# An expert loop of a mixture-of-experts trunk: the down projection moved wholly to split float32r products

## The reference

```
def swiglu(h, w_gu, w_down):
    gu = h @ w_gu                      # (rows, 1024) @ (1024, 512)
    g, u = jnp.split(gu, 2, axis=-1)
    return (jax.nn.silu(g) * u) @ w_down   # (rows, 256) @ (256, 1024)

yb = lax.map(expert_block, (xb, blk_e))    # blocks of 128 rows, one expert each
yb = yb * row_g[:, None]
return jnp.zeros((t + 1, d)).at[row_t].add(yb)[:t]
```

## Time and profile before

| | us |
|---|---|
| time, median of 3 runs | 3387.37 |
| lowest, highest | 3383.46, 3392.98 |
| the profiled execution's own time | 3384.38 |
| its span, first to last instruction | 3382.8 |
| expert loop of the first layer, about | 1000 to 1617 of the span |
| expert loop of the second layer, about | 2652 to 3268 of the span |
| mean granted TensorE clock, share of full speed | 0.939 |

### The profile page before, as it was taken

How to read it: one execution, slowest core, us unless ns; L and a number is a source line. 1 busy time by engine, 2 the same in 40 slices (tenths; PEclk the granted TensorE clock), 3 DMA queues, 4 the chain that set the end, 5 groups by cost and what they waited for, 6 DMA issues and landing times. The chain is left out here.

```text
span 3382.8 us, 41792 instructions
## 1 busy us (share of the span) xinstructions
PE 2989.3 (88%) x13540; PEld 2291.4 (68%) x13540; DVE 2044.8 (60%) x2874; ACT 1543.7 (46%) x2382; POOL 578.2 (17%) x561
## 2 busy tenths in 40 slices
PE   2899998899879999999369999988998899999983
PEld 1587776577667777777256877756776677777762
DVE  4544345544458888888345444464445788888854
ACT  0342333332337777777023323243323577777740
POOL 0000000000043333333010000000002343333320
PEclk9899999999889999999669999998998899999985
DMA  8123223123359999998321232321334799999944
GB/s 205 55 88 123 101 100 115 67 85 133 122 191 362 367 368 368 361 361 320 153 69 69 88 137 84 128 80 62 111 106 186 264 364 360 359 370 363 366 162 174
DMA packets 119233, 671.92 MB, mean 199 GB/s; under 512 B 27372, under 2 KB 28652, under 8 KB 84364
## 3 DMA queue, kind: packets, MB, share of 16 engines
q1 hardware_dynamic: 86476, 608.19, 48.9%
q0 software_dynamic: 31456, 57.70, 5.1%
q10 hardware_dynamic: 1152, 4.19, 0.3%
HBM read 655.20 MB, written 56.98 MB: 211 GB/s over the span
## 5 line engine op out<-in xcount | busy, mean ns | idle before, releaser
L1725 DVE TENSOR_TENSOR ew_lo<-ew,e_hi 128x2048 fp32r<-128x2048 f32 x256 | 586.6, 2292 | 189.1 <-ACT e_hi L1584 188.9
L659 PE MATMUL bank<-h_hi,w_hi 128*128 128x512 f32 x1248 | 513.1, 411 | 35.5 <-DVE gt L742 12.1
L1584 ACT ACTIVATE e_hi<-ew 128x2048 fp32r<-128x2048 f32 x256 | 489.9, 1914 | 104.0 <-PE bank L1870 80.1
L659 PE MATMUL bank<-h_hi,w_lo 128*128 128x512 f32 x1248 | 510.0, 409 | 0.0
L659 PE MATMUL bank<-h_lo,w_hi 128*128 128x512 f32 x1248 | 505.4, 405 | 0.0
L593 DVE TENSOR_TENSOR w_lo<-raw,w_hi 128x1024 fp32r<-128x1024 f32 x198 | 242.6, 1225 | 430.6 <-ACT w_hi L585 430.4
L1870 PE MATMUL bank<-e_hi,x_hi 128*128 128x512 f32 x1024 | 413.3, 404 | 0.0
L1870 PE MATMUL bank<-ew_lo,x_hi 128*128 128x512 f32 x1024 | 402.4, 393 | 0.0
L1870 PE MATMUL bank<-e_hi,x_lo 128*128 128x512 f32 x1024 | 400.2, 391 | 0.0
L976 ACT ACTIVATE pr<-sn,negmax 128x256 f32<-128x256 f32 (+3 forms) x256 | 138.4, 541 | 421.2 <-DVE negmax L967 421.2
L1493 POOL DMA_INDIRECT y_d<-y,idx x128 | 217.6, 1700 | 621.5 <-issue 524.0
(11 more groups left out here) (286 smaller groups left out, 4648.6 us busy)
## 6 DMA issues: line engine op xcount, KB each, us to landing
ew<-in_wexp SPq DMA_DIRECT2D x128, 2048.0 KB, 10.1
raw<-in_wmix SPq DMA_DIRECT2D x294, 512.0 KB, 4.0
ew<-in_wexp SPq DMA_DIRECT2D x128, 1024.0 KB, 10.1
yt<-y_d SPq DMA_DIRECT2D x8, 3072.0 KB, 10.1
ada<-in_ada SPq DMA_DIRECT2D x4, 2048.0 KB, 18.2
ew<-in_wexp SPq DMA_DIRECT2D x2, 3072.0 KB, 10.4
h_d<-htok ACTq DMA_DIRECT2D x8, 512.0 KB, 2.6
v_d<-vB SPq DMA_DIRECT2D x1, 3840.0 KB
```

Of the source, the lines that this page charges most:

```text
L659: ins = nc.tensor.matmul(out, lhs, rhs, start=start, stop=stop)
L1584: nc.scalar.activation(e_hi[h][:], up_part(ew, j, h), ACT.Copy).then_inc(whi_done, 1)
L1725: nc.vector.tensor_tensor(up_part(ew_lo, j, h), up_part(ew, j, h), e_hi[h][:].bitcast(F32), ALU.subtract).then_inc(wlo_done, 1)
```

## The change

All 1024 output columns of the down projection are computed with three float32r products instead of one half so and one half plain, 12 products of 512 columns for each expert. The down weights of all columns are split on ScalarE and VectorE, as two pieces of 128x1024 (one for each 128 rows of the contraction) and not one, and this split becomes the first thing that both engines do in a step. `a_hi` is rounded straight from PSUM and `a_lo` subtracted from it; the plain copy `actT` is not made in the loop. Both halves of `y` are copied out by ScalarE, between the first half of `e_hi` and `silu`; VectorE copies none. `sil` and `acted` have one buffer where they had two, so `silu(e)` waits for `gated_up(e-1)`, and `gated_up(e)` for the transposes of e-1. The waits of the other engines follow.

```diff
-            def y_half(eng, it, j):
...
-                    nc.scalar.activation(y[s][:, 0:S], bank[0][:], ACT.Copy).then_inc(yA, 1)
-                else:
-                    nc.vector.tensor_copy(y[s][:, S:D], bank[1][:]).then_inc(yD, 1)
...
                     def scatter(it, j):
                         e, s = 8 * it + j, j % 4
-                        pool.wait_ge(yA, e + 1)
-                        pool.wait_ge(yD, e + 1)
+                        pool.wait_ge(y_copied, 2 * e + 2)
...
                     def turned(it, j):
...
-                        nc.scalar.activation(actT[j % 2][:], G[j % 2][:, 0:2 * BLK].rearrange("p (f t) -> p f t", f=2),
-                                             ACT.Copy).then_inc(at_copied, 1)
-                        act.wait_ge(at_copied, e + 1)
-                        nc.scalar.activation(a_hi[j % 2][:], actT[j % 2][:], ACT.Copy).then_inc(ahi_ready, 1)
+                        nc.scalar.activation(a_hi[j % 2][:], G[j % 2][:, 0:2 * BLK].rearrange("p (f t) -> p f t", f=2),
+                                             ACT.Copy).then_inc(ahi_ready, 1)
+
+                    def down_split(it, j):
+                        e = 8 * it + j
                         act.wait_ge(dw_in[j % 4], 16 * (2 * it + j // 4 + 1))
                         if not (isinstance(e, int) and e == 0):
                             act.wait_ge(dn_ready, e)
-                        nc.scalar.activation(d_hi[:], down_part(ew, j)[:, :, 0:S], ACT.Copy).then_inc(dhi_ready, 1)
+                        for f in range(2):
+                            nc.scalar.activation(d_hi[:, f, :], down_part(ew, j)[:, f, :], ACT.Copy).then_inc(dhi_ready, 1)
+
+                    def y_rows(it, j):
+                        e, s = 8 * it + j, j % 2
+                        act.wait_ge(dn_ready, e + 1)
...
+                        for h, bank in enumerate((SB, (OB, MB))[s]):
+                            nc.scalar.activation(y[s][:, h * S:(h + 1) * S], bank[:], ACT.Copy).then_inc(y_copied, 1)
 
                     def step(it, j, first=False, last=False):
-                        if not (first and j < 2):
-                            y_half(act, it, j - 2)
+                        if not (first and j == 0):
+                            down_split(it, j - 1)
                         if not (last and j == 7):
                             x_half(e + 1, j + 1)
                         if not (first and j == 0):
                             turned(it, j - 1)
                         if not (last and j == 7):
                             w_half(e + 1, it, j + 1, 0)
+                        if not (first and j < 2):
+                            y_rows(it, j - 2)
                         silu(e, j)
...
+                    def down_split(e, j):
+                        for f in range(2):
+                            dve.wait_ge(dhi_ready, 2 * e + f + 1)
+                            nc.vector.tensor_tensor(down_part(ew_lo, j)[:, f, :], down_part(ew, j)[:, f, :],
+                                                    d_hi[:, f, :].bitcast(F32), ALU.subtract).then_inc(dlo_ready, 1)
...
                     def gate_up(e, s):
...
-                            pe.wait_ge(at_copied, e - 1)
+                            pe.wait_ge(alo_ready, e - 1)
...
                     def down(e, s):
                         pe.wait_ge(alo_ready, e + 1)
-                        pe.wait_ge(dlo_ready, e + 1)
                         if not (isinstance(e, int) and e < 2):
-                            pe.wait_ge(yA, e - 1)
-                            pe.wait_ge(yD, e - 1)
+                            pe.wait_ge(y_copied, 2 * e - 2)
...
                         for f in range(2):
-                            for i, (a, w) in enumerate(((a_hi, d_hi[:, f, :]), (a_hi, lo[:, f, 0:S]),
-                                                        (a_lo, d_hi[:, f, :]))):
-                                nc.tensor.matmul(bank[0][:], a[s % 2][:, f, :], w, start=(f, i) == (0, 0),
-                                                 stop=(f, i) == (1, 2))
-                        for f in range(2):
-                            ins = nc.tensor.matmul(bank[1][:], actT[s % 2][:, f, :], raw_w[:, f, S:D], start=f == 0,
-                                                   stop=f == 1)
+                            pe.wait_ge(dlo_ready, 2 * e + f + 1)
+                            for h, bank in enumerate((SB, (OB, MB))[s % 2]):
+                                cols = slice(h * S, (h + 1) * S)
+                                for i, (a, w) in enumerate(((a_hi, d_hi[:, f, cols]), (a_hi, lo[:, f, cols]),
+                                                            (a_lo, d_hi[:, f, cols]))):
+                                    ins = nc.tensor.matmul(bank[:], a[s % 2][:, f, :], w, start=(f, i) == (0, 0),
+                                                           stop=(f, i) == (1, 2))
```

More of the change, by code:

```diff
@@ L314, in hybrid_trunk @@
         x_lo = [place(f"x_lo{i}", [P, KD, BLK], F32R) for i in range(2)]
-        d_hi = place("d_hi", [P, 2, S], F32R)
+        d_hi = place("d_hi", [P, 2, D], F32R)
         xg = [place(f"xg{i}", [P, D]) for i in range(4)]
         y = [place(f"y{i}", [P, D]) for i in range(2)]
-        sil = [place(f"sil{i}", [P, 2 * BLK]) for i in range(2)]
-        acted = [place(f"acted{i}", [P, 2 * BLK]) for i in range(2)]
-        actT = [place(f"actT{i}", [P, 2, BLK]) for i in range(2)]
+        sil = place("sil", [P, 2 * BLK])
+        acted = place("acted", [P, 2 * BLK])
+        actT = place("actT", [P, 2, BLK], at=t_end["acted"] - 8 * BLK)
         a_hi = [place(f"a_hi{i}", [P, 2, BLK], F32R) for i in range(2)]
@@ L1587, in silu @@
                         act.wait_ge(gu_used, 2 * e + 2)
-                        if not (isinstance(e, int) and e < 2):
-                            act.wait_ge(act_done, e - 1)
-                        nc.scalar.activation(sil[j % 2][:], G[j % 2][:, 0:2 * BLK], ACT.Silu).then_inc(silu_done, 1)
+                        if not (isinstance(e, int) and e == 0):
+                            act.wait_ge(act_done, e)
+                        nc.scalar.activation(sil[:], G[j % 2][:, 0:2 * BLK], ACT.Silu).then_inc(silu_done, 1)
                     def turned(it, j):
@@ L1641, in _ @@
                             act.wait_ge(o_gu, i + 1)
-                            nc.scalar.activation(sil[0][:], G[0][:, 0:2 * BLK], ACT.Silu).then_inc(o_sil, 1)
+                            nc.scalar.activation(sil[:], G[0][:, 0:2 * BLK], ACT.Silu).then_inc(o_sil, 1)
                             act.wait_ge(o_dn, i + 1)
@@ L1729, in gated_up @@
                         dve.wait_ge(silu_done, e + 1)
-                        if not (isinstance(e, int) and e < 2):
-                            dve.wait_ge(at_ready, e - 1)
-                        nc.vector.scalar_tensor_tensor(acted[j % 2][:], sil[j % 2][:], idx[j % 8][:, 2:3].bitcast(F32),
+                        if not (isinstance(e, int) and e == 0):
+                            dve.wait_ge(at_ready, e)
+                        nc.vector.scalar_tensor_tensor(acted[:], sil[:], idx[j % 8][:, 2:3].bitcast(F32),
                                                        G[j % 2][:, 2 * BLK:], ALU.mult, ALU.mult).then_inc(act_done, 1)
@@ L1736, in turned @@
                         dve.wait_ge(ahi_ready, e + 1)
-                        nc.vector.tensor_tensor(a_lo[j % 2][:], actT[j % 2][:], a_hi[j % 2][:].bitcast(F32),
-                                                ALU.subtract).then_inc(alo_ready, 1)
-                        dve.wait_ge(dhi_ready, e + 1)
-                        nc.vector.tensor_tensor(down_part(ew_lo, j)[:, :, 0:S], down_part(ew, j)[:, :, 0:S],
-                                                d_hi[:].bitcast(F32), ALU.subtract).then_inc(dlo_ready, 1)
+                        nc.vector.tensor_tensor(a_lo[j % 2][:], G[j % 2][:, 0:2 * BLK].rearrange("p (f t) -> p f t", f=2),
+                                                a_hi[j % 2][:].bitcast(F32), ALU.subtract).then_inc(alo_ready, 1)
+                    def down_split(e, j):
[3 more added lines that the diff above has]
+                                                    d_hi[:, f, :].bitcast(F32), ALU.subtract).then_inc(dlo_ready, 1)
                     def step(it, j, first=False, last=False):
                         e = 8 * it + j
-                        if not (first and j < 2):
-                            y_half(dve, it, j - 2)
+                        if not (first and j == 0):
+                            down_split(e - 1, j - 1)
                         if not (last and j == 7):
@@ L1777, in _ @@
                             dve.wait_ge(o_sil, i + 1)
-                            nc.vector.tensor_tensor(actT[0][:], sil[0][:].rearrange("p (f t) -> p f t", f=2),
+                            nc.vector.tensor_tensor(actT[:], sil[:].rearrange("p (f t) -> p f t", f=2),
```

30 lines of the change are left out of this document (12 added, 18 removed).

## The result

The change makes the kernel slower: 3445.89 us (median of 4 runs, 3439.67 to 3455.08) against 3387.51 us for the kernel before on the same chip (4 runs), a ratio of 1.0173 with a 95% interval of 1.0146 to 1.0201. The forecast was 3394 in a range of 3350 to 3445, so the time lies a microsecond above the end of the range, at the figure that the third rival gave for L = 7.8. The profiled execution took 3439.67 us, with a span of 3438.0 and a mean granted clock of 0.932.

A forecast was written before the change was run, and what follows sets the result against it. TensorE was taken to set the expert step, DMA close behind. Shorter products -43.5, late gathers +10.8 and +37.8, first steps +10, peaks and draining -8 sum to +7: 3391 profiled, 3394 median, range 3350 to 3445.

The forecast's parts named there:

- third rival: Expert loops: the gather at its new place waits for the whole DMA queue; 3446 at L = 7.8; chance 0.20, slower.
- L: Time a gather takes from issue to landing in the expert loops; above 6.1 us it was to delay steps.
- TensorE, -43.5: Down products: 12 float32r take 2.74 us instead of 3.08, 0.34 less a step, 43.5 us over 128 steps.
- Cover of ScalarE and VectorE: Expert step: their added work stays hidden, 8.6 and 8.8 us of 9.36; a_lo is ready 0.6 us before down.
- The way of `y`, 7.1 us: ScalarE's y copies end 7.1 us after a step's opening, 4.9 us later than before, holding back scatter and gather.
- Gather start, 12.6: GpSimd issues the gather 12.6 us after a step's opening instead of 7.73, leaving 6.1 us to land.
- the formula of the forecast: Step period in the expert loops is the larger of 9.36 and (12.6 + L) / 2 us.
- L from the scatter's rows, 6.5 and 7.5: Gather landings taken from scatter medians in the first and second loop: 0.2 and 0.7 us a step, +10.8 and +37.8.
- Peaks and draining, together -8: Expert loops: landing peaks add time, stalls let the DMA queue drain; together estimated at -8 us, without a row.
- Gathers land in time: Rival for the expert loops: L stays under 6.1, giving 3344, up to 3372 with a few late; chance 0.28.
- The DMA engines are the floor: Rival: at DMA share 0.98 a step cannot fall below 9.5 us, staying near 9.7; 3380 to 3390; chance 0.10.
- The gather keeps a load's landing time: Rival: the moved gather waits for the whole queue, each us of L above 6.1 costing 60 us; chance 0.20.

The follow-up runs named there:

- e1: Changed kernel with each gather issued one expert earlier (e+4 where e+3 was), ahead of the scatter it stood behind: 3345.2 us, ratio 0.9884.
- e5: Kernel before the change with only the gather issued one expert earlier: 3388.05 us, ratio 1.0002.
- e3: Kernel before the change with only ScalarE's copy of the first half of y moved behind the first half of e_hi: 3435.04 us, ratio 1.0149.
- e8: Changed kernel with each down load halved to 512 KB, the other half of the down weights taken from a resident tile: 3364.68 us, ratio 0.9927.
- e4: Changed kernel with GpSimd's index copy made one step earlier, behind the gather of e+3: 3416.67 us, ratio 1.0087.
- e10: Changed kernel with SyncE holding each down load until a small GpSimd memset behind the gather is done: 3451.64 us, ratio 1.0123.
- e9: Changed kernel with SyncE holding each down load for a bare semaphore increment behind GpSimd's gather: 3476.4 us, ratio 1.0204.

## Why the prediction was wrong

The mechanism was the one forecast; the sum over it was 51 us short.

- **TensorE, -43.5.** Right. The 12 products take 2.74 us, an unstalled step 9.35 (forecast 9.36), and e1 against e5 gives -40 us.
- **Cover of ScalarE and VectorE.** Right. Besides the gathers, TensorE's waits in the two windows shown above are only 1.1 us and 0.4 us, once each, and in e1 none of the 56 steps is over 9.38 us. Once in each loop, behind the last expert, where no gate/up products are left to cover it, TensorE waits 4.0 us for `a_lo`; the kernel before has a wait of 3.4 us at that place. `a_hi` from PSUM took 385 ns and `a_lo` 417.
- **The way of `y`, 7.1 us.** Right: 7.0, and the scatter at 8.6.
- **Gather start, 12.6.** Too early by 0.5 us: 13.1. The unchanged index copy, 0.22 us before, takes 1.85 at its new place, which the scatter's own operation, 0.93 us where it was 1.86, pays back in part. Half a microsecond is worth 0.25 us in a step, 27 us over 110 steps, by the formula of the forecast.
- **L from the scatter's rows, 6.5 and 7.5.** 6.6 in the first loop, which is right, and 6.4 in the second, 1.1 us less than was taken. The step that the prediction called its weakest held. It is luck that the errors of start and L cancel: (13.1 + 6.6) / 2 - 9.35 = 0.50 and (13.1 + 6.4) / 2 - 9.35 = 0.40, over 54 steps each 48.6 us; the forecast's two terms add up to the same 48.6.
- **Peaks and draining, together -8: the step that failed.** The stalls cost 98 us (the changed kernel against e1); the forecast had 10.8 + 37.8 + 10 - 8 = 51. (In the first steps of the first loop, for which it had landings of 10.2 us, the gathers landed in 6.8 to 7.5.) I had let the medians stand for all gathers, and set the spread against the draining. But a gather that lands early gives nothing back, and one that is late alone delays TensorE by the whole of its lateness, not by half. This can be worked out from the landing times of the 58 gathers of the first loop: each step opens 9.35 us after the last one, or 13.1 + L after the last but one, whichever is later. With 6.6 for every L this gives 9.84 us a step, with each gather's own L 10.03; measured are 10.18. So 0.49 of the 0.83 us lost in a step is the median, 0.19 the spread, and 0.15 the rest. Two more readings of the same trace take up half of that rest: the transposes start 0.14 us behind a landing, which adds 0.05, and some gathers start later than 13.1, up to 15.9 after a stall, which adds 0.03. For e3 the same reckoning gives 10.09, where the medians gave 9.5 and 10.21 were measured; for e8 9.52 instead of 8.95, measured 9.59; for e4, with its start of 10.2, 9.92 and measured 10.07; for e1 9.35, measured 9.35.
- **What the 98 us are made of.** From the page of e1:

```profile
PE 2949.1 (88%) x13796; PEld 2345.0 (70%) x13796; DVE 2112.3 (63%) x2874; ACT 1655.3 (50%) x2510; POOL 660.8 (20%) x561
```

These are the 13796 matmuls of the changed kernel. The span is 97.8 us shorter (3340.2 against 3438.0) and TensorE's busy time 30.1 us. So 67.7 us of the loss are idle time and 30.1 are the same products taking longer when they come in pieces. The clock is at most half of the latter: in the changed kernel's two loops the granted clock is 0.50 for 29.6 us in all, and half of that is 15 (2.1 us of the step of 16.71 shown above are such time beyond the wait). The other half is open; the shown duration of the last product ahead of each gap, 0.39 us where 0.23 is its cost in a stream, may be part of it. Against the kernel before, the busy time of e1 is 40.2 us less, the price of the products once more.
- **Draining** exists (83 GB/s in the window after the stall), but it comes after the damage, and the stretches as a whole still stand at a DMA share of 0.93.

**The rivals.** *Gathers land in time* did not happen; its 3344 is what e1 reaches by another way. *The DMA engines are the floor* is refuted at 9.5 us and above by the 378 GB/s and the steps of 9.35 of e1. It was not far off: by its own reckoning the 3.55 MB of a step take 9.4 us at 378 GB/s, an estimate, and in e1 the loads do fall behind. *The gather keeps a load's landing time* had the right time, 3446, by the wrong numbers: it wanted L = 7.8, and L was 6.6. It was nearer in kind, and the steps of over 10 us that were to be its sign did come (10.18): 31 of the 51 gathers of 1072 to 1590 land within 1 us behind the load issued ahead of them, 0.3 us behind it in the rows above. The Trainium skill (DMA: Bandwidth & Descriptors, section on queues, rings and completion order) says that an engine takes turns between its queue rows packet by packet, by which the small gather should overtake (of 64 rows four go to an engine, not the three of the forecast). The trace of the changed kernel does not agree with what I drew from that: landing is 6.6 us in the median, and 4.8 only where 512 KB less stand ahead of it. The trace of e1 does agree. Of the issues in its 1100 to 1500, with the median time to landing in us:

```profile
ew<-in_wexp SPq DMA_DIRECT2D x43, 1024.0 KB, 18.3
xg<-h_d,idx POOLq DMA_INDIRECT x43, 9.4
```

There a gather is issued 3.3 us behind the down load and lands, in the median, 4.1 us ahead of it, 41 of 43 ahead. So a gather neither waits for all that was issued before it nor passes it freely. What remains open is why: e10, meant to part the place in the order from the amount in flight, moved the other load too, and a run with both loads behind the gather was not made.

The chance of 0.35 for slower was taken from the ends of L alone. The reckoning above could have been done before the change was run. Over the scatter landings of the kernel before, whose ends and medians shows, with the forecast's own start of 12.6 and 9.36 us of TensorE, it gives steps of 9.99 us in the first loop and 10.40 in the second. Over 60 steps of each that is some 100 us, and 3387 - 43.5 + 100 = 3444, an estimate that would have put the likeliest case at slower.

## What to carry to other kernels

A step that is moved moves everything behind it in the in-order streams that wait for it: here a copy moved by 5 us held a scatter, and the scatter a prefetch that does not depend on it. Put a prefetch ahead of such a wait; with that one edit the change gains 1.2% instead of losing 1.7%, and 3345.2 us (e1) beats both kernels. When a transfer has just enough time by its median, do not reckon with the median: take the list of landing times, let each late one count in full and each early one for nothing, and carry the openings forward step by step. And where a share of 0.98 leaves open whether the DMA engines are full, look whether the landing times of the loads grow along the loop.

## What the runs showed of the hardware

In these traces an operation of GpSimd that reads the on-chip memory stands still while VectorE runs an operation with two inputs there. The index copy has 216 ns in the kernel before, in the first of these groups, and 1862 in e1, in the second:

```profile
L1463 POOL COPY idx<-slots 128x4 int32 x48 | 10.3, 216 | 0.0
```

```profile
L1451 POOL COPY idx<-slots 128x4 int32 x48 | 89.4, 1862 | 0.0
```

In the step shown above it starts at 1227.39, 0.42 us into VectorE's L1726, and ends at 1229.30; L1726 ends at 1229.26. In 55 of the 56 steps of the first loop the copy ends 0.04 us after L1726. The Trainium skill (SBUF — State Buffer, section on who interferes with whom) says that a VectorE instruction with two SBUF inputs contends with a GpSimd instruction that reads SBUF, and that the later one is blocked in full; the trace agrees, 1.91 us against 0.22. In e4 the gather's own operation, put in the copy's place, took 2.16 us: VectorE's L1733 ended at 1211.61, and the gather's operation 0.90 us later, about what one takes that is not held up (0.96 in e9).

A bare semaphore increment behind an indirect DMA on GpSimd fires when that operation begins and not when it ends: in e9 the operation starts at 1204.65 and lasts 0.96 us, and the load that waits for the increment is issued at 1204.67; over 1072 to 1590 it is never more than 0.19 us behind the start. And a core that was at 366 GB/s with TensorE as the pace reached 378 in e1, in steps 3.6% shorter, so the DMA share of 0.98 did not say how much was left: it was at least 3%. What told the two apart is the landing time of the loads, which stayed at 8 to 12 us in the first loop before and grew from 8.0 to 20.1 in e1.
